# Modulation vectors of a two-block transformer: TensorE accumulation against VectorE chains, on one Trainium2 core

## What is computed

```python
c_act = jax.nn.silu(c)
for i in range(DEPTH_2):
    mod = (c_act @ mod_w[i] + mod_b[i]).reshape(B, 6, D)[:, :, None, :]
    hin = x * (1.0 + mod[:, 1]) + mod[:, 0]
    ...
    x = layer_norm(DEEPNORM_ALPHA * x + mod[:, 2] * y, ln_g[i, 0], ln_b[i, 0])
    hin = x * (1.0 + mod[:, 4]) + mod[:, 3]
    y = conv_ffn(hin, ffn_w_in[i], ffn_conv_w[i], ffn_conv_b[i], ffn_w_out[i])
    x = layer_norm(DEEPNORM_ALPHA * x + mod[:, 5] * y, ln_g[i, 1], ln_b[i, 1])
```

## Time and profile before

| | us |
|---|---|
| median of 3 runs | 958.13 |
| lowest and highest | 956.78, 958.15 |
| the profiled execution | 956.92 |
| its span, first to last instruction | 955.1 |
| PE busy | 912.6 |
| DVE busy | 655.5 |
| ACT busy | 452.0 |
| POOL busy | 94.7 |

### The profile page before, as it was taken

One profiled execution on the slowest core, in us unless ns is written; L12 is line 12 of the kernel. 1 busy time (PEld: TensorE's weight loads), 2 busy tenths in 40 slices (PEclk: granted clock), 3 DMA queues, 4 the chain that ended last, 5 costly groups with the idle time before them and its releaser, 6 DMA issues. The chain is left out here.

```text
span 955.1 us, 15038 instructions
## 1 busy us (share of the span) xinstructions
PE 912.6 (96%) x6056; PEld 778.5 (82%) x6056; DVE 655.5 (69%) x1049; ACT 452.0 (47%) x714; POOL 94.7 (10%) x67
## 2 busy tenths in 40 slices
PE   8999999999999799989999999989999899999992
PEld 7887878667767587769999999768997799999991
DVE  4587566575656777679958667877777876566556
ACT  4463544444434555445545444354554655454530
POOL 2000001000000211013101210030000221001013
PEclk9999999999999799999999999999999999999997
DMA  8976455455877473257967779648705875646301
GB/s 300 353 239 211 155 182 172 127 170 167 291 282 249 169 274 102 89 206 266 367 202 265 281 245 365 206 143 308 253 3 202 308 306 186 209 154 214 121 1 44
DMA packets 56190, 200.23 MB, mean 210 GB/s; under 512 B 6413, under 2 KB 7349, under 8 KB 56121
## 3 DMA queue, kind: packets, MB, share of 16 engines
q1 hardware_dynamic: 55816, 198.21, 59.8%
q0 software_dynamic: 304, 1.06, 0.3%
HBM read 198.18 MB, written 1.06 MB: 209 GB/s over the span
## 5 line engine op out<-in xcount | busy, mean ns | idle before, releaser
L1066 PE MATMUL ps<-XT,wsp 128*128 128x256 f32 x768 | 217.7, 283 | 2.8 <-DVE XT L1349 1.5
L1067 PE MATMUL ps<-XT,wsp 128*128 128x256 f32 x768 | 214.5, 279 | 0.0
L1068 PE MATMUL ps<-XT,wsp 128*128 128x256 f32 x768 | 214.2, 279 | 0.0
L1306 DVE TENSOR_TENSOR wsp<-ring,wsp 128x1024 fp32r<-128x1024 f32 x137 | 173.2, 1274 | 25.4 <-ACT wsp L1837 25.2
L1837 ACT CAST wsp<-ring 128x1024 fp32r<-128x1024 f32 (+1 forms) x136 | 141.9, 1047 | 88.7 <-PE ps L1068 77.4
L1066 PEld LDWEIGHTS ps<-XT,wsp 128*128 128x128 f32 x768 | 144.0, 187 | 8.8 <-issue 5.0
L1067 PEld LDWEIGHTS ps<-XT,wsp 128*128 128x128 f32 x768 | 143.9, 187 | 0.9
L1068 PEld LDWEIGHTS ps<-XT,wsp 128*128 128x128 f32 x768 | 143.8, 187 | 0.0
L1066 PE MATMUL ps<-wsp,ra 128*128 128x512 f32 x244 | 97.7, 400 | 2.9 <-issue 1.1
L1068 PE MATMUL ps<-wsp,ra 128*128 128x512 f32 x244 | 96.9, 397 | 0.0
L1067 PE MATMUL ps<-wsp,ra 128*128 128x512 f32 x244 | 96.4, 395 | 0.0
(11 more groups left out here) (262 smaller groups left out, 1567.0 us busy)
## 6 DMA issues: line engine op xcount, KB each, us to landing
ring<-in_mod_w SPq DMA_DIRECT2D x48, 512.0 KB, 4.7
arena<-in_mod_w SPq DMA_DIRECT2D x43, 512.0 KB, 5.6
ring<-in_ffn_a SPq DMA_DIRECT2D x29, 512.0 KB, 4.9
ring<-in_ffn_b SPq DMA_DIRECT2D x25, 512.0 KB, 4.6
ring<-in_ffn_o SPq DMA_DIRECT2D x23, 512.0 KB, 4.6
arena<-in_ffn_o SPq DMA_DIRECT2D x21, 512.0 KB, 4.7
arena<-in_ffn_b SPq DMA_DIRECT2D x19, 512.0 KB, 4.8
arena<-in_ffn_a SPq DMA_DIRECT2D x15, 512.0 KB, 4.8
```

What stands on the lines that cost most here:

```text
L1066: pe.matmul(o, l[0], r[0], start=start, stop=False)
L1067: pe.matmul(o, l[0], r[1], start=False, stop=False)
L1068: return pe.matmul(o, l[1], r[0], start=False, stop=stop)
L1306: ve.tensor_tensor(w[:, 1024:1024 + n], raw[slot[0]][:, 0:n], w[:, 0:n].bitcast(f32), SUB).then_inc(*done("V", "lo", u, also=[("raw", *slo ...
```

## The change

It has three parts, and what follows from them.

1. **Layer 0's four column vectors become DVE chains.** `modulation` now makes `mod_v` steps for all eight vectors, and the task starts with the mLSTM instead of at the head of the kernel. Layer 0 uses the two rows of `R2` as accumulators, since these are free until the first row vector. Its rate is 0.8 tiles a unit on layer 0.
2. **Column sums in four column groups.** At the end of a chain one `mod_one` step on PE multiplies the accumulator with a stationary block of ones, 32 columns on each of the four column groups: the shape of one `mod_k`. ACT copies it (`mod_sum`) and PE transposes it (`mod_pe`), for all eight vectors. `mod_pv` is gone.
3. **Row vectors spread through DRAM.** `mod_row` on DVE adds the bias to the PSUM sum, 128x256, and POOL then issues two DMAs: four rows of 256 to a DRAM scratch, and from there to all 128 partitions of `R2`. POOL waits for the first before it issues the second. L1160 and L1375 are gone.

With them (0,2) moves from x1 to m00, so that x1 has no tiles now and m00 has eight. The tiles of (0,5) are loaded to six regions that come free at the end of the MLA attention, where before they were loaded earlier. Some semaphores of the mLSTM are shared, for which nothing else changes.

In the fences below the rows of before carry the lines of before, and those of after the lines of after: L1076, L1077 and L1078 of after are L1066, L1067 and L1068 of before, L1089 is L1079, L1159 is L1149, L1307 is L1306, and L1521 and L1525 of after are L1525 and L1529 of before. In L1366 and L1368 (`mod_v`) R is the accumulator in `R2`, arena or ring the weight tile, cactr the vector `c`.

The diff, cut to its core:

```diff
-MOD_PACE = [0.52, 0.52, 0.52, 0.52, 0.4, 0.5, 0.5]
+MOD_PACE = [0.8, 0.4, 0.5, 0.5]
...
-    sums, accs = {q: None for q in range(3)}, {}
-
-    def vector_end(i, m, q, on_pe, b):
-
-        if on_pe:
-            add("mod_sum", i, m, b, q, sums[q])
-            bank.put(b[0])
+    sums, accs = {q: None for q in range(3)}, {0: None, 1: None}
+
+    def columns_end(i, m, q):
+
+
+        b = bank.get()
+        add("mod_one", i, m, q, b, prior("bank", b))
+        accs[q] = ("mod_one", i, m)
+        add("mod_sum", i, m, b, q % 2, sums[q % 2])
+        bank.put(b[0])
         yield
-        is_row, r = m in (2, 5), 0 if m == 2 else 1
-        while i and is_row and ("r2", r) not in have:
+        b = bank.get()
+        add("mod_pe", i, m, b, prior("bank", b), q % 2)
+        sums[q % 2] = ("mod_pe", i, m)
+        bank.put(b[0])
+        add("mod_fin", i, m)
+        have.add(("mod", i, m))
+        yield
+
+    def rows_end(i, m, b):
+
+        while i and ("r2", 0 if m == 2 else 1) not in have:
             yield
-        br = load(("row", "mod_b", i * 6144 + m * 1024)) if is_row else None
-        if is_row:
-            yield
-        for cb in range(2 if is_row else 1):
-            b = bank.get()
-            add("mod_pe" if on_pe else "mod_pv", i, m, cb, b, prior("bank", b), br, q)
-            (sums if on_pe else accs)[q] = ("mod_pe", i, m, cb)
-            bank.put(b[0])
-        if is_row:
-            free_raw(br)
-        else:
-            add("mod_fin", i, m)
+        br = load(("bias", 2 * i + m // 5), 256)
+        yield
+        add("mod_row", i, m, b, br, sums[2])
+        sums[2] = ("mod_out", i, m)
+        bank.put(b[0])
+        free_raw(br)
         have.add(("mod", i, m))
         yield
...
-            if i == 0:
-                b = bank.get()
-            elif n == 4:
-                while 0 not in accs:
-                    yield
+            q = n % 2 + 2 * i
+            while q not in accs:
+                yield
             for k in range(8):
                 s = soon.pop(0)
                 if k < 7:
                     soon.append(load(("mod_w", (i * 6 + m) * 8 + k + 1)))
                 elif n + 1 < len(vectors):
                     soon.append(load(("mod_w", (vectors[n + 1][0] * 6 + vectors[n + 1][1]) * 8)))
-                if i == 0:
-                    add("mod_k", i, m, k, s, b, prior("bank", b))
-                else:
-                    add("mod_v", i, m, k, s, accs[n % 2], n % 2)
+                add("mod_v", i, m, k, s, accs[q], q)
                 free_raw(s)
                 yield
-            for _ in vector_end(i, m, n % 2, i == 0, b if i == 0 else None):
+            for _ in columns_end(i, m, q):
                 yield
...
-            between.append(vector_end(self.i, self.m, 2, True, self.b))
+            between.append(rows_end(self.i, self.m, self.b))
...
-    mod = W.beside(modulation(), MOD_PACE[0])
-
+    mod = []
...
+    mod.append(W.beside(modulation(), MOD_PACE[0]))
...
     tbl = W.beside(tables(), 1.0)
-    v = Between(0, 2, [(SIDE, None), (SIDE + 1, None), (SIDE + 2, ("ix_sel", 1))] +
-                [(SIDE + 3 + n, [("gated", 1, 0), ("gated", 1, 1), ("tr", "hm1", 2)]) for n in range(4)], 1, 1.3)
     proj_a("mx", 12, "w_out", 6, 1, lambda t, cb, b: add("ev_wo", t, 1, b), True)
-    v.tiles(3)
-    transposed("x1", 8, None, apart=True, filled=(lambda: v.tiles(2), lambda: v.tiles(3)))
-    v.end()
+    transposed("x1", 8, None, apart=True)
+    vs = []
+
+    def before_gate(cb, q):
+        if (cb, q) == (1, 0):
+            free = [("gated", 1, 0), ("gated", 1, 1), ("tr", "hm1", 2)]
+            vs.append(Between(0, 2, [(SIDE, ("mod_one", 0, 3)), (SIDE + 2, ("ix_sel", 1)), (SIDE + 7, ("fin_dsa", 3))] +
+                              [(SIDE + 3 + n, free) for n in range(4)], 1, 2.0))
+
...
+    proj_a("x1", 8, "w_gate", 0, 2, ev_gate, True, before_gate)
...
-    modulated(0, 0)
+    modulated(0, 0, vs.pop(), (3, 3, 2))
...
-    proj_a("ot0", 8, "mla_o", 0, 2, lambda t, cb, b: resid(0, 0, t, cb, b), True, with_heads(0, mt))
+
+    def before_mla_o(cb, q):
+        with_heads(0, mt)(cb, q)
+        if (cb, q) == (1, 0):
+            vs.append(Between(0, 5, [(SIDE + 1, ("mod_one", 0, 4))] + [(SIDE + 8 + n, ("fin_o", 0, 7)) for n in range(6)],
+                              1, 2.0))
+
+    proj_a("ot0", 8, "mla_o", 0, 2, lambda t, cb, b: resid(0, 0, t, cb, b), True, before_mla_o)
     mla_end = ("fill", *bank_last(steps))
     add("ln_fin", 0, 0, 1, 512)
-    mod[1] = MOD_PACE[4]
-    modulated(0, 1, v, (3, 3, 2))
-    accs[0] = accs[1] = ("mod_k", 0, 5, 7)
+    mod[0][1] = MOD_PACE[1]
+    accs[2] = accs[3] = mla_end
+    modulated(0, 1, vs.pop(), (3, 3, 2))
...
-        acc = [arena[:, 12818:13842], arena[:, 13842:14866]]
+        acc = [R2[:, 0, :], R2[:, 1, :], arena[:, 12818:13842], arena[:, 13842:14866]]
...
                     ins.then_inc(*done("P", "mod_k", i, m, k, also=[("raw", *s)]))
+                elif kind == "mod_one":
+                    i, m, q, b, before = a
+                    for e in new("P", ("mod_v", i, m, 7), ("cst2",), before):
+                        pe.wait_ge(*e)
+                    for j in range(4):
+                        ins = pe.matmul(ps[b[0]][32 * j:32 * j + 32, 0:256], ones[:, 0:32],
+                                        acc[q][:, j * 256:(j + 1) * 256], start=True, stop=True,
+                                        tile_position=(0, 32 * j))
+                    ins.then_inc(*done("P", "mod_one", i, m))
                 elif kind == "mod_pe":
-                    i, m, cb, b, before, br, q = a
-                    total = msum[q]
+                    i, m, b, before, q = a
                     for e in new("P", ("mod_sum", i, m), ("cst",), before):
                         pe.wait_ge(*e)
-                    if br is not None:
-                        for j in (2 * cb, 2 * cb + 1):
-                            ins = pe.matmul(ps[b[0]][:, (j % 2) * 256:(j % 2) * 256 + 256],
-                                            bass.AP(cst, 32 * j, [[NCONST, 128], [0, 128]]), total, start=True, stop=True)
-                    else:
-                        for k in range(2):
-                            ins = pe.transpose(ps[b[0]][:, k * 128:(k + 1) * 128], total[:, k * 128:(k + 1) * 128], ID)
-                    ins.then_inc(*done("P", "mod_pe", i, m, cb))
-                elif kind == "mod_pv":
-                    i, m, cb, b, before, br, q = a
-                    total = acc[q]
-                    for e in new("P", ("mod_v", i, m, 7), ("cst2",), before):
-                        pe.wait_ge(*e)
-                    if br is not None:
-                        ins = pe.matmul(ps[b[0]], ones[:, 0:128], total[:, cb * 512:(cb + 1) * 512], start=True, stop=True)
-                    else:
-                        for k in range(8):
-                            ins = pe.matmul(ps[b[0]][:, k:k + 1], total[:, k * 128:(k + 1) * 128], ones[:, 0:1],
-                                            start=True, stop=True)
-                    ins.then_inc(*done("P", "mod_pe", i, m, cb))
+                    for k in range(2):
+                        ins = pe.transpose(ps[b[0]][:, k * 128:(k + 1) * 128], msum[q][:, k * 128:(k + 1) * 128], ID)
+                    ins.then_inc(*done("P", "mod_pe", i, m))
                 elif kind == "grow":
                     b, before = a
...
-                        ve.tensor_tensor(o_, x, b_, ADD).then_inc(*done("V", "mod_ev", i, m, 0, also=[("bank", *b)]))
+                elif kind == "mod_row":
+                    i, m, b, br, before = a
+                    for e in new("V", ("mod_k", i, m, 7), ("ld", *br), before):
+                        ve.wait_ge(*e)
+                    ve.tensor_tensor(msum[2], ps[b[0]][:, 0:256], raw[br[0]][:, 0:256], ADD).then_inc(
+                        *done("V", "mod_row", i, m, also=[("bank", *b), ("raw", *br)]))
+                elif kind == "mod_pe":
+                    i, m, b, _, _ = a
+                    for e in new("V", ("mod_pe", i, m), ("cols",)):
+                        ve.wait_ge(*e)
+                    y = {0: 0, 1: 8, 3: 16, 4: 24}[m]
+                    o_, b_ = grid(MC[i][:, y:y + 8], 4), grid(K("mod_b", i * 48 + m * 8, 8), 4)
+                    ve.tensor_tensor(o_, ps[b[0]][:, 0:256].rearrange("p (c j r) -> p j c r", c=2, j=4)[:, :, :, 0], b_,
+                                     ADD).then_inc(*done("V", "mod_ev", i, m, 0, also=[("bank", *b)]))
                 elif kind == "mod_fin" and a[1] in (1, 4):
                     i, m = a
                     n, x = 2 * i - 1 + (m == 4), {1: 8, 4: 24}[m]
...
+                elif kind == "mod_row":
+                    i, m = a[0:2]
+                    r = 0 if m == 2 else 1
+                    for e in new("G", ("mod_row", i, m)):
+                        po.wait_ge(*e)
+                    po.dma_start(rows[r], bass.AP(msum_t[2], 0, [[32 * 256, 4], [1, 256]])).then_inc(
```

(5 more changed lines are left out.)

49 lines of the change are left out of this document (14 added, 35 removed).

## The result

The changed kernel takes 936.1 us (median of 4 runs, 933.9 to 937.9) against 958.0 before: a ratio of 0.9775, with a 95% interval of 0.976 to 0.979. The forecast was 922 in a range of 915 to 932. The sign was right and the range missed by 4 us: from 958.0, 22 us were won where 922 needed 36. (The sum itself started at the profiled execution's 956.9 and so held 34.9; the median it is now set against lies 1.1 us higher.) The profiled execution took 937.85 us, with a span of 936.0.

The account below looks back on a forecast made before the run. The prediction took PE's instructions as the bound, with DVE keeping up. From the profiled 956.9 us, the terms for removed and added work summed to 920.3, with new waits 922; the range was 915 to 932.

Parts of the forecast that it names:

- (a): Layer 0's column vectors: their 32 `mod_k` leave PE, 0.76 us each, -24.3 us.
- (b): The first `mod_k` of layer 0: PE's wait for its tile, which had not landed, goes, -1.5 us.
- (c): The four row vectors: spread without PE, 1.72 us each, -6.9 us; POOL's DMAs taken as 0, ends 0 and +2.
- (d): Layer 1's chains: the four sums by L1175 go, 1.79 us each, -7.2 us.
- (e): Chain ends in both layers: eight `mod_one` come on PE, 0.76 us each, +6.1 us.
- (f): Four more sums are copied by ACT and transposed by PE, 0.27 us each, +1.1 us.
- (g): x1: it loses its eight tiles, -3.1 us, or -2 if DVE comes to X late.
- (h): m00: it gets the eight tiles, half clock goes, second weight unit comes earlier, -0.8 us; other end -3.3.
- (i): New waits of PE from 32 more chain tiles on DVE: +2 us, ends 0 and +6.4.
- DVE becomes the bound for a part: Rival: softmax chains, low halves and tiles share DVE's queue, X late at x1, clock falls there; 928 to 931 us, chance 0.18.
- rival of slower: Rival: each `mod_v` holds the `lo` behind it and PE waits; loses from 1.14 us per tile, 961 at 1.28; chance 0.03.

Follow-up runs that it names:

- e3_nok: The kernel before with 28 of the 32 `mod_k` of layer 0's column vectors left out, with their tiles' loads: 937.9 us.
- e11_cols: The kernel before with only the column sums in column groups added, for layer 1's four column vectors: 953.6 us.
- e4_pe0: The changed kernel with layer 0's four column vectors again made by 32 `mod_k` on PE, the other parts as changed: 945.6 us.
- e2_thin: The changed kernel with 28 of layer 0's 32 chain tiles cut to 64 of 1024 columns on DVE: 925.9 us.
- e6_mla: The changed kernel with chain tiles beginning at 60 us, stopping before hm1's copy, and five tiles of (0,4) with its `mod_one` moved behind m00: 928.3 us.
- e13_nolow: The changed kernel with the same 32 chain tiles, none ahead of hm1's copy, at x1's copy, at m00 or ahead of cq's copy: 927.7 us.
- e1_hold: The changed kernel with tiles k=4 to 6 of vector (0,3) behind hm1's transposed copy in DVE's queue, not ahead of it: 932.8 us.

## Why the prediction missed

The sum without new waits was 920.3, the forecast 922, the measurement 936.1. By the steps, as the prediction has them:

- **(a)** 24.3 forecast, 21.3 read, 18.3 for 28 of them measured in e3_nok. The count was right (L1159 has 32 steps). The price failed: I took 0.76 us from a place between two products for all 32, and 14 of them stand where PE changes to another operation anyway, which makes 0.57.
- **(b)** right: without it the first sixteen product steps need 2.2 us less (e3_nok), which is 0.76 and the 1.5.
- **(c)** 6.9 forecast, 6.2 measured. Spreading costs what the earlier trace rows show. The bound of +2 for GpSimd's queue was the right thing to keep: its gain row now stands behind a wait for DRAM, starts at 441.01 and runs beside DVE's instructions, which take about twice as long (1.28 and 1.21 us alone), and PE waits 0.8 us at 448:
```profile
440.43 0.56 POOL L2166 DMA_DIRECT2D R<-rows  x1 [4.80 <-DMA rows<-msum]
441.01 3.65 POOL L2180 TENSOR_TENSOR X<-X,ring 128x1024 f32<-128x1024 f32 x1
444.63 2.27 POOL L2205 TENSOR_TENSOR ra<-wk,ra 128x512 fp32r<-128x512 f32 x1
```
```profile
442.90 2.83 DVE L1368 SCALAR_TENSOR_TENSOR arena<-arena,cactr 128x1024 f32<-128x1024 f32 x1
445.66 2.32 DVE L1307 TENSOR_TENSOR wsp<-ring,wsp 128x1024 fp32r<-128x1024 f32 x1
447.90 1.21 DVE L1307 TENSOR_TENSOR wsp<-arena,wsp 128x1024 fp32r<-128x1024 f32 x1
```
- **(d), (e), (f)** for the second block 3.1 forecast, 3.8 measured (e11_cols).
- **(g)** right: x1 takes 2.7 us, with 0.79 idle, and the clock stays at 1.00 there:
```profile
272.73 1.91 PE L1089 MATMUL ps<-cst,X 128*128 128x128 f32 x16
275.43 0.47 PE L1076 MATMUL ps<-wsp,XT 128*128 128x512 f32 x1 [0.79 <-issue]
```
- **(h)** right as far as it went. The second unit starts 13.0 us after the gate's last product, where I had 13 to 13.5, and the clock is 1.00 to there. But I stopped the sum at that product. It waited 1.92 us for its low half, and in this execution the clock fell behind that wait. Rows of the changed kernel:
```profile
313.77 0.69 DVE L1350 TENSOR_TENSOR XT<-wk,XT 128x512 fp32r<-128x512 f32 x1 [1.66 <-ACT XT L1872]
314.38 2.35 DVE L1307 TENSOR_TENSOR wsp<-ring,wsp 128x1024 fp32r<-128x1024 f32 x2
```
```profile
315.66 0.50 PE L1076 MATMUL ps<-wsp,XT 128*128 128x512 f32 x1 [1.92 <-DVE wsp L1307]
316.63 0.63 PE L1076 MATMUL ps<-wsp,XT 128*128 128x512 f32 x1
```
To the start of the third unit m00 takes 17.5 us; before, it took 17.0. So -0.8 was +0.4, and +1.9 in e4_pe0 with its wait for `mod_sum`. But the half clock is 1.5 of the 17.5 us and does not come each time: the same stretch takes 1.5 us less in e2_thin, e6_mla and e13_nolow, with the same wait at full clock. There (h) is worth -1.1.
- **(i)** the step that failed: 2 forecast, an upper end of 6.4, 10.2 measured (e2_thin). I took DVE's share of a stretch and the units of `hi` and `lo` made ahead as the buffer. Both held for most ordinary products, which wait for weights, though not behind three tiles in a row (2.65 us in e1_hold). A transposed copy can't be made ahead: it is made from data that has just been finished, every product behind it needs it, and what stands in front of it in DVE's queue counts in full. So does a `mod_one` set right behind the last tile of its chain. The change put two tiles in front of hm1's copy. The order of DVE's instructions shows them there, and I had looked at it for m00 alone. The half clock behind such a wait, 2.5 us at hm1, was in the forecast for m00 only.

The 14.1 us between forecast and measurement thus split into 8.2 for (i), 10.2 less the 2 that were allowed, and 5.6 that e2_thin leaves (the rest, 0.3, is 922.3 rounded to 922). Of the 5.6, (a) is 3.0, and (c) 0.7 less the 0.7 that (d) to (f) gave more. The start of the sum is 1.1: it is 956.9, and the median before is 958.0. Another 1.1 is the wait at hm1's copy, which e2_thin has at 2.18 us and the kernel before at 1.06. What is left, 0.4 us, the runs can't tell from nothing. Neither part alone leaves the range: 920.3 with 10.2 for (i) is 930.5, and 936.1 with (i) at 2 is 927.9. Together they miss it by 4 us, and (i) is the larger.

The rival "DVE becomes the bound for a part" named the engine and the clock, but priced it by load (928 to 931), and load it was not: e13_nolow has the same load and took 927.7 against 936.1. The rival of slower asked for 1.14 us of delay for each tile; it was 10.2 / 32 = 0.32.

The rule of the Trainium skill ("SBUF — State Buffer", section "Who interferes with whom") fits the doubled rows at 442.90 and 445.66, with GpSimd busy from 441.01 to 446.90 beside both. It explains none of the waits at 230 and 286 us, where GpSimd does nothing.
